# A hybrid diffusion step: the long convolution's transforms split by symmetry, on sums and differences of mirrored tokens

## The reference

```python
z = sum(zp[:, j:j + L] * conv_w[j] for j in range(SHORT_CONV)) + conv_b
x0, x1, v = jnp.split(z, 3, axis=-1)
u = x1 * v
hc = _hyena_filter(L, ...)                 # 2L taps, forward and backward, per channel
uf = jnp.fft.rfft(u, n=2 * L, axis=1)
hf = jnp.fft.rfft(hc, n=2 * L, axis=0)
y = jnp.fft.irfft(uf * hf[None], n=2 * L, axis=1)[:, :L] + u * d_bias
return x0 * y
```

## Time and profile before

| | us |
|---|---|
| runs, median (lowest to highest) | 1976.92 (1970.02 to 1981.5) |
| the profiled execution's own time | 1972.32 |
| its span | 1970.5 |
| TensorE busy in it | 1852.7 |

### The profile page before, as it was taken

The page is one execution under the profiler, slowest core; times in us unless marked ns, Lnnn a source line. Parts: engine busy times, 40 slices in busy tenths (PEclk is TensorE's granted clock), DMA queues, the critical chain, the costliest instruction groups (busy, mean ns, idle before and its releaser), DMA issues.

```text
span 1970.5 us, 27375 instructions
## 1 busy us (share of the span) xinstructions
PE 1852.7 (94%) x9586; PEld 1300.1 (66%) x9586; DVE 1546.3 (78%) x2334; ACT 1155.4 (59%) x1543; POOL 303.6 (15%) x141
## 2 busy tenths in 40 slices
PE   4999999969999999999999999997999999999996
PEld 1776777846666666666667787785566666666663
DVE  4543646679999999999876364666899999999996
ACT  2410256238777777778652115733677777777773
POOL 0100031110212222122102003011022122221200
PEclk9999999979999999999999999998999999999998
DMA  9569200259999999999763722033999999999984
GB/s 342 172 224 334 86 1 23 107 211 429 394 376 381 377 387 385 382 369 391 287 206 131 258 84 87 1 118 140 395 412 389 378 379 376 372 390 385 386 297 161
DMA packets 86476, 542.14 MB, mean 275 GB/s; under 512 B 7057, under 2 KB 9875, under 8 KB 61829
## 3 DMA queue, kind: packets, MB, share of 16 engines
q1 hardware_dynamic: 75908, 504.54, 65.4%
q0 software_dynamic: 10496, 36.64, 6.8%
HBM read 517.63 MB, written 23.53 MB: 275 GB/s over the span
## 4 chain that ended last, share of the span: by engine, by line
PE 85%; DVE 7%; DMA 3%; ACT 2%; issue 2%; POOL 1%; SPq 0%; DVEq 0%; ACTq 0%; POOLq 0%
PE bank L1146 52%; PE bank L829 11%; PE bank L1006 4%; PE bank L707 2%; PE bank L954 2%; PE bank L969 1%; PE bank L1163 1%; PE bank L865 1%; DMA ring<-in_exp_w 1%; PE bank L939 1%; PE bank L1044 1%; PE bank L1027 1%; PE bank L1156 1%; PE bank L1077 1%; PE bank L725 1%
## 5 line engine op out<-in xcount | busy, mean ns | idle before, releaser
L1444 ACT ACTIVATE arena_h_r<-ring 128x1024 fp32r<-128x1024 f32 x480 | 503.9, 1061 | 167.8 <-PE bank L1146 149.1
L2028 DVE TENSOR_TENSOR ring_r<-ring,arena_h_r 128x1024 fp32r<-128x1024 f32 x470 | 557.0, 1218 | 28.4 <-ACT arena_h_r L1444 21.5
L1146 PE MATMUL bank<-arena_h_r,arena_u_r 128*80 128x512 f32 x1280 | 373.2, 398 | 9.3 <-DVE arena_u_r L2048 9.3
L2028 DVE TENSOR_TENSOR ring_r<-ring,arena_u_r 128x1024 fp32r<-128x1024 f32 x282 | 333.4, 1219 | 13.0 <-ACT arena_u_r L1444 7.5
L1444 ACT ACTIVATE arena_u_r<-ring 128x1024 fp32r<-128x1024 f32 x288 | 300.7, 1059 | 59.3 <-PE bank L1146 59.3
L1146 PE MATMUL bank<-ring_r,arena_u_r 128*80 128x512 f32 x1024 | 318.9, 392 | 0.0
L1146 PEld LDWEIGHTS bank<-arena_h_r,arena_u_r 128*80 128x80 f32 x1280 | 188.4, 151 | 105.0 <-DVE arena_u_r L2048 7.8
L1146 PE MATMUL bank<-arena_u_r 128*80 128x512 f32 x768 | 216.9, 391 | 0.0
L1146 PEld LDWEIGHTS bank<-ring_r,arena_u_r 128*80 128x80 f32 x1024 | 152.2, 149 | 85.2 <-issue 1.4
L1146 PE MATMUL bank<-arena_h_r,arena_z_r 128*80 128x512 f32 x640 | 182.0, 399 | 3.6 <-DVE arena_z_r L2063 3.6
L659 POOL DMA_INDIRECT arena_z<-xn_dram,icur x32 | 134.9, 4215 | 307.0 <-issue 276.2
(11 more groups left out here) (285 smaller groups left out, 2653.7 us busy)
## 6 DMA issues: line engine op xcount, KB each, us to landing
ring<-in_exp_w SPq DMA_DIRECT2D x192, 2048.0 KB, 10.2
ring<-in_ada_w SPq DMA_DIRECT2D x24, 2048.0 KB, 9.0
ring<-in_w_in SPq DMA_DIRECT2D x8, 2048.0 KB, 18.0
ring<-in_w_out SPq DMA_DIRECT2D x2, 4096.0 KB, 13.2
x_res<-arena_z POOLq DMA_DIRECT2D x10, 512.0 KB, 2.9
xn_dram<-arena_u POOLq DMA_DIRECT2D x10, 512.0 KB, 2.9
arena_z<-x_res POOLq DMA_DIRECT2D x5, 512.0 KB, 4.4
arena_z<-in_x_sample SPq DMA_DIRECT2D x4, 512.0 KB, 6.3
```

Source lines behind the costliest of these rows:

```text
L1146: mm = pe.matmul(bank[out + n][0:CAP, :], xs[:, c, :], w[:, n * 512:(n + 1) * 512], start=(c == 0 and part == 0), stop=(c == KC - 1 and pa ...
L1444: act.activation(high[c], slot[s][:, c, :], ACT.Copy).then_inc(high_ready, 1)
L2028: v.tensor_tensor(slot_r[s][:, c, :], slot[s][:, c, :], high[c], ALU.subtract).then_inc(low_ready, 1)
```

## The change

The latent tokens' transforms use that the tables are symmetric about the middle token. VectorE forms sums and differences of mirrored tokens (`folded`: first half plus or minus the second half reversed) at the end of `conv(4)` and `conv(5)`; both u tiles are then transposed from these. The forward step multiplies sums and differences by one combined table each (`fwd_t`, cos+sin and cos-sin, 512x512) with 4 products for a frequency tile instead of 8. The inverse computes two halves for a token tile pair with 8 products instead of 16 and VectorE joins them by a sum and a difference; the far half comes out in reversed token order. So x0 of token tiles 2 and 3 is turned by a product with a reversed identity (`turn`, 128x128) and copied by ScalarE a second time, and the transposes of these two tiles before the output projection multiply by `turn` for the convolution's columns. The filter spectrum is computed for even frequencies alone from even and odd taps (16 products instead of 32), and VectorE joins the halves (`halves_joined`, four 128x512 operations at step 1 of the loop).

The order moves too: keys and queries are all transposed before the gate products, the gate comes next, then the turned x0, then u, whose transposes now wait for the gate's results. The forward step waits for u's copies. `turn` is loaded before the output weights. The steps in the loop are at other places. The context's transforms are as they were.

```diff
-        filc, fils = slot[0][:, 0:4, 0:512], slot[0][:, 4:8, 0:512]
-        dftc, dfts = slot[0][:, 0:4, 512:1024], slot[0][:, 4:8, 512:1024]
+        filc, fils = slot[0][:, 0:4, 0:HY], slot[0][:, 4:8, 0:HY]
+        fwd_t, inv_t = slot[0][:, 0:4, 512:1024], slot[0][:, 4:8, 512:1024]
...
-        FILL_AT = {0: [0], 1: [1], 3: [2], 4: [3], 6: [4], 7: [5], 9: [6], 10: [7], 11: [8], 14: [9], 15: [10], 16: [11],
-                   17: [12], 18: [13], 20: [14], 21: [15], 23: [16], 24: [17]}
+        FILL = ([("fwd", j, j < 4) for j in range(NT)]
+                + [("inv", 0, 0), ("inv", 0, 1), ("inv", 4, 2), ("inv", 1, 0), ("inv", 1, 1)])
+        FILL_AT = {0: [0], 2: [1], 4: [2], 6: [3], 8: [4], 12: [5], 13: [6], 15: [7], 17: [8], 19: [9]}
+        Y_ORDER = [0, 3, 4, 1, 2]
...
-        YSQ_AT = {18: 0, 19: 1, 21: 2, 24: 3, 27: 4}
+        YSQ_AT = {17: 0, 18: 1, 20: 2, 23: 3, 24: 4}
...
-                sp.wait_ge(x0_mm, l * 3 + 3)
+                sp.wait_ge(x0_mm, l * 4 + 3)
+                sp.dma_start(turn, i["turn"]).then_inc(turn_in, 16)
                 sp.wait_ge(ut_mm, l * 3 + 3)
                 sp.dma_start(slot[2], i["w_out"][l].rearrange("(c p) n -> p c n", p=P)).then_inc(wo_in, 16)
-                sp.dma_start(turn64, i["turn64"]).then_inc(turn_in, 16)
...
-                        for j in range(2):
-                            jj = 2 * (g % 2) + j
-                            for a in range(4):
-                                mm = pe.matmul(out[:, j * HY:(j + 1) * HY], table[:, a, jj * P:(jj + 1) * P],
-                                               taps[:, a, :], start=(a == 0), stop=(a == 3))
+                        at = slice(g % 2 * P, (g % 2 + 1) * P)
+                        for a in range(4):
+                            mm = pe.matmul(out[:, a // 2 * HY:(a // 2 + 1) * HY], table[:, a, at], taps[:, a, :],
+                                           start=(a % 2 == 0), stop=(a % 2 == 1))
...
-                for j in range(4):
+                for j in range(7):
                     qk_transposed(j)
...
-                for j in range(4, 7):
-                    qk_transposed(j)
+                pe.wait_ge(turn_in, l * 16 + 16)
+                pe.wait_ge(qk_a, l * 7 + 7)
+                pe.matmul(bank[6][:, :], turn, x0tok[:, 2:4, :].rearrange("p t n -> p (t n)"), start=True, stop=True)\
+                    .then_inc(x0_mm, 1)
+                pe.wait_ge(u_done, l + 1)
+                for g in range(3):
+                    pe.wait_ge(gm_out, l * GH + g + 1)
+                    conv_transposed(bank[UT[g]], g, 2).then_inc(ut_mm, 1)
...
+                            even, odd = (0, 2) if j < 2 else (2, 0)
+                            for a in range(2):
+                                pe.matmul(out[:, 0:HY], fwd_t[:, a, j * P:(j + 1) * P], utok[:, even + a, :],
+                                          start=(a == 0), stop=(a == 1))
+                            for a in range(2):
+                                mm = pe.matmul(out[:, HY:2 * HY], fwd_t[:, 2 + a, j * P:(j + 1) * P], utok[:, odd + a, :],
+                                               start=(a == 0), stop=(a == 1))
...
                             for a in range(4):
-                                mm = pe.matmul(out[:, 0:HY], (dfts if x else dftc)[:, a, t * P:(t + 1) * P],
-                                               prod[2 * x][:, a, :], start=(x == 0 and a == 0), stop=(x == 1 and a == 3))
+                                plus = (a < 2) == (x == 0)
+                                at = (0 if plus else HY) + j * P
+                                mm = pe.matmul(out[:, x * HY:(x + 1) * HY], inv_t[:, a, at:at + P],
+                                               prod[0 if plus else 2][:, a, :], start=(a == 0), stop=(a == 3))
...
+                        if n in (4, 5) and t in (2, 3):
+                            mm = pe.matmul(dst, zt[:, t, a:a + P], turn, start=True, stop=True)
+                        else:
+                            mm = pe.transpose(dst, zt[:, t, a:a + P], ident)
...
+                act.wait_ge(x0_mm, l * 4 + 4)
+                act.activation(x0tok[:, 2:4, :], bank[6][:, :].rearrange("p (t n) -> p t n", t=2), ACT.Copy).then_inc(x0_out, 1)
...
-                        v.tensor_tensor(conv_lat[m - 2], conv_lat[m - 2], conv_lat[4], ALU.mult)
+                        link(v.tensor_tensor(conv_lat[m - 2], conv_lat[m - 2], conv_lat[4], ALU.mult))
+                        front, back = conv_lat[m - 2][:, 0:256], conv_lat[m - 2][:, 256:512][:, ::-1]
+                        v.tensor_tensor(folded[m - 4][:, 0:256], front, back, ALU.add)
+                        v.tensor_tensor(folded[m - 4][:, 256:512], front, back, ALU.subtract)
...
+                def halves_joined():
+
+                    v.wait_ge(spec_out, l * 5 + 5)
+                    for f, at in enumerate(halves_at):
+                        e, o = at[:, 0], at[:, 1]
+                        v.tensor_tensor(sres[:, f, 0:2, :], e, o, ALU.add)
+                        x, y = (e, o) if f == 0 else (o, e)
+                        ins = v.tensor_tensor(sres[:, f, 2:4, :], x, y, ALU.subtract)
+                    link(ins)
...
+                        near, far = zt[:, j, 1024:1280], zt[:, 3 - j, 1024:1280]
+                        link(v.tensor_copy(near, bank[3][:, 0:HY]))
+                        v.tensor_tensor(far, near, bank[3][:, HY:2 * HY], ALU.subtract)
+                        link(v.tensor_tensor(near, near, bank[3][:, HY:2 * HY], ALU.add))
+                        for t in (j, 3 - j):
+                            v.tensor_tensor(zt[:, t, 1024:1280], zt[:, t, 1024:1280], x0tok[:, t, :], ALU.mult)\
+                                .then_inc(yh_done, 1)
...
+                    if n == 1:
+                        halves_joined()
```

More of the change, by code:

```diff
@@ L891, in _ @@
                     conv_transposed(bank[X0T[g]], g, 0).then_inc(x0_mm, 1)
[L892 to L897, removed]
                 pe.wait_ge(late_in, l * 64 + 64)
@@ L913, in qk_transposed @@
                     mm.then_inc(qk_mm, 1)
-                for j in range(4):
+                for j in range(7):
                     qk_transposed(j)
+                for e in "av":
+                    s, per, v = taken(max(n for n in range(NP_) if proj[n][2] == e))
+                    pe.wait_ge(s, l * per + v)
                 for h in range(GH):
-                    if h < 3:
-                        pe.wait_ge(ut_out, l * 3 + h + 1)
-                    else:
+                    if h == 3:
                         pe.wait_ge(spec_out, l * 5 + 5)
@@ L931, in dft @@
                         out = bank[2 + j % 2]
-                        if j == 0 and x == 0:
+                        if j == 0:
+                            pe.wait_ge(ut_out, l * 3 + 3)
                             pe.wait_ge(dft_in, l * 32 + 32)
                             pe.wait_ge(gm_out, l * GH + GH)
-                        if j >= 2 and x != 1:
+                        if j >= 2:
                             pe.wait_ge(prod_out, l * 5 + j - 1)
-                        if x < 2:
-                            for a in range(4):
-                                mm = pe.matmul(out[:, x * HY:(x + 1) * HY], (dfts if x else dftc)[:, a, j * P:(j + 1) * P],
-                                               utok[:, a, :], start=(a == 0), stop=(a == 3))
+                        if x:
+                            even, odd = (0, 2) if j < 2 else (2, 0)
[5 more added lines that the diff above has]
+                                               start=(a == 0), stop=(a == 1))
                         else:
@@ L1767, in _ @@
                         .then_inc(gm_out, 1)
+                for g in range(3):
+                    w = 2 if g < 2 else 1
+                    v.wait_ge(ut_mm, l * 3 + g + 1)
+                    v.tensor_copy(utok[:, 2 * g:2 * g + w, :], bank[UT[g]][:, 0:w * HY].rearrange("p (t n) -> p t n", t=w))\
+                        .then_inc(ut_out, 1)
+                def halves_joined():
[6 more added lines that the diff above has]
+                    link(ins)
                 def dft_taken(k):
                     kind, j, x = FILL[k]
-                    if kind == "fwd" and x:
+                    if kind == "fwd":
                         src = bank[2 + j % 2]
                         v.wait_ge(fwd_mm, l * 5 + j + 1)
-                        v.wait_ge(spec_out, l * 5 + 5)
                         for n, (a, f) in enumerate(((0, 0), (1, 1), (0, 1), (1, 0))):
@@ L2168, in tables @@
         whole = np.pi / n * np.outer(k, k + 0.5)
-        c[f"dft{name}_cos"], c[f"dft{name}_sin"] = np.cos(half), np.sin(half)
-        c[f"fil{name}_cos"], c[f"fil{name}_sin"] = np.cos(whole), np.sin(whole)
+        if n == LAT:
+            even = np.arange(0, n, 2)
+            freq = np.concatenate([even, n - 1 - even])
+            taps = np.concatenate([even, even + 1])
```

(8 more changed lines are left out.)

73 lines of the change are left out of this document (40 added, 33 removed).

## The result

The changed kernel takes 1945.38 us (median of 4 runs, 1943.18 to 1947.92), against 1975.66 for the kernel before on the same chip (4 runs, 1970.02 to 1981.5). The ratio is 0.9842, with a 95% interval of 0.9825 to 0.9859. That is 30.3 us less, where 35.2 were forecast; 1938 stood for 1945.4. The profiled execution took 1943.18 with a span of 1941.0.

What follows compares the result with a forecast made beforehand. TensorE was taken as the bound until the last filled-in step, then ScalarE and VectorE share it. Gains of 16.7 us (layer 1) and 18.5 (layer 0), 35.2 in all, gave 1937.1 or 1940 us; forecast 1938, range 1924 to 1954.

Steps and rivals of the forecast that it cites:

- Filter to first forward step: From the filter's first product to the loop's first forward step: starts 6.1 us earlier, ends 4.7 and 7.7.
- the late x0: Rival: `turn` takes 13.7 us to load, ScalarE's loop starts 8 us later a layer; gain 19, 1953 us; chance 0.03.
- Step 4: Loop: `halves_joined` puts four VectorE operations ahead of the first products and second pair's reductions; TensorE waits 0.8 us.
- Steps 10 to 12: Loop, narrow context block: 2.4 us of TensorE waits, the last for GpSimd's combination at about 1205.1.
- the waits that go: Loop: about 3 us of old waiting disappears, the 4.9 before the first inverse step less small work done in it.
- Step 22: Loop: the second inverse join on VectorE, like the first, makes TensorE wait 1.0 us.
- Step 16: Loop: first join, five VectorE operations and two waits ahead of the reductions freeing score banks; TensorE waits 2.1 us.
- The rival "slower": Loop steps 0 to 26, both layers: waits halve TensorE's clock; up to 70 us lost a layer, about 2079; chance 0.04.
- the forecast gain of 1.0: Layer 0's first inverse step: a shorter wait recovers 1.0 of the 1.4 us lost at half clock.
- The end of the loop: After the filled-in steps: 0.7 us for ScalarE's closer squares and 0.4 for two-instruction products, a loss of 1.1 us.
- Layer 0's modulation load: Layer 0, TensorE's 3.33 us wait for the last modulation weights: smaller tables ahead gain 0.8 us, between 0 and 3.3.
- The bound of 7.7 us: Upper end for filter to first forward step if only TensorE counts: 6.9 saved, 0.9 added, 1.7 of waiting gone.

Runs made afterwards that it cites:

- the joins' experiment: Changed kernel with VectorE taking the two inverse joins later and ScalarE's last two squares following the second: 1940.31 us, ratio 0.9831.
- the last experiment: Changed kernel with layer 0's last modulation load issued ahead of the forward and inverse tables instead of behind them: 1942.72 us, ratio 0.9838.
- the one with the filter twice: Changed kernel with every filter product issued twice, 64 instead of 32 a layer; its time lies under the expected 1958 to 1959 us.
- priced by doubling: Three runs of the changed kernel with every filter, forward or inverse product issued twice; layer 1's stretch grew by 6.6, 6.2 and 5.8 us.

## Why the prediction was right, and where it was off

The direction and the mechanism held: TensorE bounds the stretch, half of three groups of products leave it, and part of the gain turns into waits for VectorE at the places named. By its steps:

**Filter to first forward step: 6.1 forecast, 6.2 measured.** The chain in layer 1 shows 6.91 us for 32 products, as forecast:

```profile
1149.21 6.91 PE bank L877 x32
...
1163.57 0.86 PE bank L933 x2
...
1164.90 1.62 DVE ring L1796 x3
```

The turned x0 takes 0.86 (four at 0.216), u's copies 1.62 (forecast 1.5). Each landmark fell within 0.2 us of the walk. `turn` landed 1.7 us after its issue (1.9 in layer 0), so the late x0 did not come about.

**Step 4: 0.8 forecast, 0.67 measured. Steps 10 to 12: 2.4 forecast, 0.71 and 0.36 measured**, 1.3 too much charged, of which the waits that go take back a part: they were put at about 3 us, and the trace of the kernel before has 2.41 (1.77 and 0.64) ahead of its first inverse step. Hence the first inverse product at 38.9 us after the filter's start instead of "about 40". **Step 22: 1.0 forecast, 1.00 measured.**

**Step 16: 2.1 forecast, 3.35 measured, and this is the term that was mis-sized.** The walk gave the first join its five operations and two waits (1.9 us, as the joins' experiment confirms), but took VectorE's other operations at their old durations. The 128x8 addition, held by GpSimd, took 1.76 us: 1.60 more than alone, and 1.32 more than in the kernel before, where it took 0.44. The Trainium skill, "SBUF — State Buffer", section "Who interferes with whom", states just this: a VectorE instruction with both inputs in SBUF contends with a GpSimd instruction that reads SBUF, and the one that comes second is blocked until the first has ended, whatever its size. This case's traces agree wherever such a pair is shown above (ends at 1194.98 and 1201.98 against GpSimd's 1194.94 and 1201.95, and the two of the kernel before). In the kernel before, the addition came at 1218.82, 1.1 us ahead of the first rounding (1219.89), and met only a combination of 0.73 us; in the changed one at 1193.22, 5.2 us behind it (1187.98). The prediction let the roundings move with the first inverse step and dismissed them with "the slack they had"; slack was the wrong question, the overlap was the right one, and the subtraction of 1.05 us in the trace of the kernel before could have raised it.

**The clock.** The rival "slower" had the right place, the loop after its waits, and its price came due on a small scale: 1.5 us in layer 1 and 2.6 in layer 0, by the windows above. The argument against it rested on a longest wait of 2.1 us. The Trainium skill, "TensorE: Matmul & The Clock Gate", section "HAM oscillation — how this bites in real kernels", describes a kernel whose clock falls at every wait between its bursts. That does not appear here: the third part's mean clock is 0.97, and of the waits of 0.67 to 1.18 us in the loop none is followed by half clock. In layer 0 the forecast gain of 1.0 from a first inverse step at full clock did come: eight products in 1.99 us where the earlier trace rows had 3.42. But the half clock reappeared ten microseconds later, at step 16, and took back more than it had given.

```profile
254.19 1.99 PE L973 MATMUL bank<-ring 128*128 128x256 f32 x8 [0.36 <-POOL ring L647]
```

**The end of the loop: 1.1 forecast, 0.2 measured.** From step 26's scores to the projection it is 30.0 us before (1250.85, in the earlier trace rows, to 1280.83) and 30.1 after (1219.62 to 1249.76). ScalarE's closer squares did not reach TensorE.

**Layer 0's modulation load: 0.8 forecast, nothing measured.** It lands 8.8 us after its issue in both kernels; the smaller tables in front of it did not matter, as the last experiment shows too. Layer 0's filter even began 0.95 us later in the profiled execution (215.45 against 214.50). That is within what the executions do by themselves: in the other kernels above, leaving out the last, which alone touches something ahead of the filter, it began between 211.3 and 216.9. TensorE's timelines show one reason, the last modulation step at half or at full clock, here the changed kernel after a wait of 3.37 us and then the one with the filter twice after 2.93:

```profile
198.56 3.60 PE L718 MATMUL bank<-ring,cs 128*32 128x512 f32 x16 [3.37 <-DMA ring<-in_ada_w]
```

```profile
196.12 1.92 PE L718 MATMUL bank<-ring,cs 128*32 128x512 f32 x16 [2.93 <-DMA ring<-in_ada_w]
```

The balance of layer 1's third part, which came out 2.7 us longer than forecast: 1.25 from the longer wait at step 16, 1.5 from the clock, 0.9 less at the loop's end; the remaining 0.85 lies scattered over the walk of steps 16 to 26, and no term names it. With the first two parts (1.0 gained over the forecast) that makes 15.0 instead of 16.7. In layer 0 it is 15.7 instead of 17.7, the clock's 2.6 being larger there. The terms priced by doubling come to 18.6 us in layer 1 (6.6 + 6.2 + 5.8) against the 22.3 that the prediction took off TensorE (6.9 + 15.4): 3.7 us of them filled waits, or met a milder clock. The step from 18.6 to the 15.0 measured must be what the change adds, new waits above all; no run prices that by itself.

Three slips of the working do not carry the forecast. The bound of 7.7 us counts 1.7 us of waiting ahead of the loop, where TensorE was idle for 0.79. A gain of 28 us is 1944 in one place and 1947 in another, which start from different times. And 0.6, 0.15, 0.16 and 0.02 add up to 0.93, not 0.92.

What stays open is when the clock falls. It fell behind 1.75 us of waiting in both layers of one kernel, behind 1.45 in one layer and not in the other of the next, and in the kernel before the same wait at the first inverse step had 0.50 in layer 0 and 1.00 in layer 1. What else enters was not tried.

## What to carry to other kernels

When work leaves the bounding engine, lay the timelines of all engines over each other at their new offsets: here an operation of 8 columns on VectorE took as long as what was left of GpSimd's instruction, 1.76 us instead of 0.16. Price a wait twice, for its length and for the clock behind it. And where a small operation or a join stands ahead of what frees a bank, reorder that engine's own queue first; with GpSimd's turn it gave 3.4 to 4.4 us a layer here, with no arithmetic changed.

## What the runs showed that was not expected

- A 128x8 addition on VectorE with two operands in SBUF took 1.76, 0.63 or 0.16 us, by how much of a GpSimd rounding (2.32 us) was left when it came; the reciprocal behind it, with one operand, took 0.20 each time.
- Six products of no use, in a wait of 3.35 us, left a wait of 0.78 and saved 1.5 and 2.6 us of half clock.
- The same 2 MB load lands in 8.6 us ahead of 2 MB of tables and in 8.3 to 8.8 behind them, while the tables' own landing goes from 6.5 and 8.7 to 11.1 and 13.7.
